# Experts in interleaved group order, and the first 128 rows of three experts computed beside the routing of the last tile

## The chip, the cores and the metric

One core of a Trainium2 chip. The metric is device time in microseconds (us) of one execution of the program; lower is better.

## What is computed

One layer over 4096 prompt tokens and 128 sample tokens of width 1024, in float32: a norm, one input projection, a Mamba-2 scan beside a gated MLP, an output projection with residual, then a mixture of experts. Its routing decides the order of everything at the end of the program:

```python
g_sel = jnp.argmax(g_logits, axis=-1)                       # 1 of 4 groups
top_val, top_idx = lax.top_k(e_sel_logits, TOP_K_IN_GROUP)  # 2 of the 8 experts of that group
weights = p_group * jax.nn.softmax(top_val, axis=-1)
expert_idx = g_sel[:, None] * EXPERTS_PER_GROUP + top_idx
# per expert, in blocks of 128 rows:
(silu(xb @ w_gate[e]) * (xb @ w_up[e])) @ w_down[e]         # 1024 -> 256 -> 1024
x = x + moe                                                 # then a last RMSNorm
```

Both experts of a token lie in one group. With these inputs the 8448 (token, expert) pairs fill 79 blocks of at most 128 rows over 32 experts.

## The kernel before

**Phase 1** (`pe_phase1`, `over_tiles`) goes over 33 tiles of 128 tokens; tile 32 is the sample (T = 4224 rows). Each turn projects tile i+1 and finishes tile i. The order on each engine is written out by hand, with semaphores between engines. For a finished tile the kernel stores the residual rows x2 and the normed rows h2 in DRAM; `dve_route` picks the two experts, `pe_rank` and `dve_slots` give each pair a slot, and `pool_scatter` writes token number and weight into that slot of `slot_d`, which has a list of T slots for each expert. The two last turns are `tn.sample` (turn 32) and `tn.end` (turn 33): no projection is left, so PE has only the output projection of the sample (L457), the ranks (L525, L526) and the updates of the sample's states (L549, `pe_sample_update`, eight pieces).

**The tables** (`dve_tables`) can be made only when the last tile has its ranks: from the counts (`carry`) VectorE works out how many blocks each expert has, which list row each of the blocks reads (`row_i`, then one gather `list_rows`), and for each block the slot of its weights in SBUF (`tcol`, `tab`). PE turns both by transposes (`pe_table_rows`, L1685 and L1692).

**Phase 2** (`over_pairs`) goes over the blocks, 80 here, in order of experts 0 to 31. A block b is: `gather(b)` of 128 rows of h2 by POOL; the transpose of those rows, made by ACT and DVE (`move`, `turn`), except for blocks 0 and 1, whose rows PE transposes itself (`pe_rows`, L1639); gate and up products (`pe_gate_up`, L1657, 8 matmuls written, 16 in the trace, in two halves); `silu` and `gate`; the transpose of the hidden rows (`pe_hidden`, L1667) and its copy (`hidden`, L1744); `pe_down` (L1676); `weigh` (L1797) on DVE, which scales by the routing weight and adds the residual row. A token's first expert writes its sum back into the x2 rows by `keep(b)`, and its last one reads it by `earlier(b)`, adds it (`add_first`, L1805), takes the last norm (`squares`, `root_of`, `norm`, L1791) and stores the row (`store`). PE's step b does gate and up of block b+1 around the hidden rows of block b, then the down product of b, so the last step also computes gate and up of a block 80 that nobody uses.

POOL issues all gathers and scatters. Its step b: `keep(b-1)`, `residual(b+1)`, `gather(b+5)`, `root_of`, `earlier(b)`, `store(b-2)`. `earlier(b)` waits until `keep(b-1)` has landed, since a row it reads can have been written by any block before. SP loads the weights of an expert (2 MB gate and up, 1 MB down) into one of four slots (`sp_phase2`), and in phase 1 the first three (`load_first`). DVE's step b: `weigh(b-1)`, `turn(b+2)`, `gate(b+1)`, `norm`, `add_first(b-1)`.

## Time and profile before

| | before |
|---|---|
| median of 3 runs | 2767.61 us (2767.44 to 2770.74) |
| the profiled execution | 2770.37 us |
| its span, first to last instruction | 2768.6 us |
| mean granted clock of TensorE | 0.993 |
| busy: PE, DVE, ACT, POOL | 2719.4, 1916.3, 1453.6, 818.5 us |

The span is what the rows of the trace lie in; the 1.8 us between it and the execution's time belong to its start and end. PE is TensorE's matmuls, PEld its weight loads, DVE is VectorE, ACT ScalarE, POOL GpSimd, SP the engine that issues most plain DMAs. A granted clock of 1.0 is 2.4 GHz, 0.5 is 1.2 GHz. "idle before <-releaser" is the time that an engine stood still before an instruction, and what ended it.

### The profile page before, as it was taken

The numbers are of one execution on the slowest core, as the hardware profiler recorded it, in microseconds if no ns is written. First come the engines' busy times: TensorE is split into PE (matmuls) and PEld (weight loads), VectorE is DVE, ScalarE is ACT, GpSimd is POOL, SyncE is SP. The second block draws the span as 40 slices with busy tenths as digits, with TensorE's granted clock in tenths as the row PEclk, the third lists the DMA queues.
The fourth block names the chain that finished last, engine by engine and source line by source line (L and its number), as shares of the span: only waits on it lengthen the run. The fifth ranks groups of instructions, "written<-read, shape, count | busy, mean of one in ns | idle before, by whom it ended". The sixth has DMA issues, their size and how long they took to land.

```text
span 2768.6 us, 38299 instructions
## 1 busy us (share of the span) xinstructions
PE 2719.4 (98%) x11649; PEld 1761.8 (64%) x11649; DVE 1916.3 (69%) x5154; ACT 1453.6 (53%) x3363; POOL 818.5 (30%) x1368
## 2 busy tenths in 40 slices
PE   8999999999999999999999999997999999999997
PEld 6777777767777777677767776773444444444443
DVE  5777777776777776767777767675666666666665
ACT  2445444554455445544554455444666666666665
POOL 1021112111211121112111211113565655656655
PEclk9999999999999999999999999998999999999999
DMA  8212211211121112111221121157888677778864
GB/s 322 94 62 77 62 46 47 77 62 46 47 76 62 47 47 77 61 47 47 72 66 46 46 76 62 50 197 281 302 285 293 239 264 267 280 256 294 319 212 145
DMA packets 109137, 377.90 MB, mean 136 GB/s; under 512 B 37201, under 2 KB 38866, under 8 KB 98930
## 3 DMA queue, kind: packets, MB, share of 16 engines
q1 hardware_dynamic: 48450, 236.13, 24.2%
q0 software_dynamic: 60480, 139.24, 15.0%
q8 instruction: 102, 1.67, 0.3%
q14 instruction: 105, 0.86, 0.1%
HBM read 326.14 MB, written 123.03 MB: 162 GB/s over the span
## 4 chain that ended last, share of the span: by engine, by line
PE 94%; DVE 2%; DMA 2%; issue 1%; ACT 1%; SPq 0%; POOL 0%; DVEq 0%; POOLq 0%; ACTq 0%
PE PB L369 24%; PE PB L1657 20%; PE PB L380 16%; PE PB L457 11%; PE SS L1676 5%; PE TB L1676 5%; PE YB L457 4%; PE YB L411 2%; DMA arena<-in_w_in 1%; PE SS L420 1%; PE SS L424 1%; PE TB L433 1%; PE YB L1667 1%; PE MB L402 1%; DVE xc L817 0%
## 5 line engine op out<-in xcount | busy, mean ns | idle before, releaser
L369 PE MATMUL PB<-arena,hT 128*128 128x512 f32 (+2 forms) x2112 | 727.7, 498 | 3.5 <-DVE x_res L937 2.2
L1657 PE MATMUL PB<-arena,hT 128*128 x1296 | 582.5, 592 | 0.0
L369 PEld LDWEIGHTS PB<-arena,hT 128*128 128x128 f32 x2112 | 397.7, 191 | 272.0 <-issue 222.4
L380 PE MATMUL PB<-hT,arena 128*128 128x128 f32 x4224 | 487.7, 277 | 4.7 <-DVE arena L1146 4.7
L380 PEld LDWEIGHTS PB<-hT,arena 128*128 128x128 f32 x4224 | 482.2, 193 | 8.6 <-issue 4.9
L1657 PEld LDWEIGHTS PB<-arena,hT 128*128 128x128 f32 x1296 | 240.2, 190 | 271.0 <-issue 271.0
L1183 POOL TENSOR_SCALAR rs<-sq 128x2 f32<-128x2 f32 (+1 forms) x66 | 14.0, 213 | 1238.5 <-ACT h L744 886.5
L457 PE MATMUL PB<-arena,tT 128*128 128x274 f32 (+1 forms) x1056 | 358.0, 493 | 0.3 <-ACT tT L638 0.3
L457 PEld LDWEIGHTS PB<-arena,tT 128*128 128x128 f32 x1056 | 195.6, 190 | 139.7 <-issue 120.5
L1787 DVE TENSOR_TENSOR gv<-ycat,PB 128x256 f32<-128x256 f32 x81 | 34.1, 421 | 288.9 <-ACT ycat L1739 288.9
L817 DVE SCALAR_TENSOR_TENSOR xc<-xT,cols,xc 128x128 f32<-128x128 f32 x792 | 216.8, 346 | 3.5
L744 ACT ACTIVATE h<-x_res 128x1024 f32<-128x1024 f32 x33 | 34.9, 1056 | 297.5 <-DVE x_res L937 297.5
L1744 ACT ACTIVATE xdt<-YB 128x256 f32<-128x256 f32 x80 | 30.6, 383 | 280.8 <-PE YB L1667 280.8
L630 ACT ACTIVATE yb<-ycat 32x128 f32<-32x128 f32 x384 | 118.1, 308 | 52.5 <-DVE ycat L928 48.4
L1676 PE MATMUL TB<-arena,xdt 128*128 x320 | 143.9, 592 | 0.0
L1676 PE MATMUL SS<-arena,xdt 128*128 x320 | 143.8, 592 | 0.0
L590 ACT ACTIVATE xT<-PB 128x512 f32<-128x512 f32 x64 | 38.3, 598 | 198.9 <-PE PB L380 198.2
L630 ACT ACTIVATE zz<-ycat 32x128 f32<-32x128 f32 x384 | 117.8, 307 | 35.1 <-DVE ycat L906 30.9
L1731 ACT ACTIVATE zz<-x_in 32x256 f32<-32x256 f32 x320 | 132.1, 413 | 3.9
L457 PE MATMUL YB<-arena,tT 128*128 128x274 f32 x528 | 127.6, 394 | 0.0
L1553 POOL DMA_INDIRECT xT<-x_rows,bc x81 | 98.7, 1219 | 68.6 <-DMA x_rows<-x_res,bc 43.6
L815 DVE TENSOR_SCALAR xc<-xT,cols 128x128 f32<-128x128 f32 x264 | 70.8, 342 | 66.2 <-issue 66.2
(292 smaller groups left out, 4204.1 us busy)
## 6 DMA issues: line engine op xcount, KB each, us to landing
arena<-in_w_expert SPq DMA_DIRECT2D x32, 2048.0 KB, 9.9
arena<-in_w_expert SPq DMA_DIRECT2D x32, 1024.0 KB, 6.5
h_rows<-h SPq DMA_DIRECT2D x34, 512.0 KB, 6.0
x_in<-in_x_rows SPq DMA_DIRECT2D x33, 512.0 KB, 4.3
hT<-in_x_cols SPq DMA_DIRECT2D x33, 512.0 KB, 3.7
x_res<-in_x_rows SPq DMA_DIRECT2D x33, 512.0 KB, 3.5
dec<-running_sums SPq DMA_DIRECT2D x33, 512.0 KB, 3.8
x_rows<-x_res SPq DMA_DIRECT2D x33, 512.0 KB, 5.2
```

Source lines behind the costliest of these rows:

```text
L369: mm = nc.tensor.matmul(out, hT[u][:, k, :], w_group(name)[:, k, :], start=k == 0, stop=k == KD - 1)
L380: mm = nc.tensor.matmul(PB[b][:, c * P:(c + 1) * P], w_block(name, c)[:, k, :], hT[u][:, k, :], start=k == 0, stop=k == KD - 1)
L411: mm = nc.tensor.matmul(bank[:, c], decay[:, h, :], xdt[:, c], start=True, stop=True)
L457: mm = nc.tensor.matmul(out_p[b], tT[:, k, :], w_out_sb[b][:, k, :], start=k == 0, stop=k == KD - 1)
L590: ins = nc.scalar.activation(xT[u][:, half(b), HALO:], PB[b][:, :].rearrange("p (k t) -> p k t", k=4), ACT.Copy)
L630: ins = nc.scalar.activation(rows_moved[b][32 * q:32 * (q + 1), g * P:(g + 1) * P], rows_quarter(b, g, q), ACT.Copy)
L815: ins = V.tensor_scalar(dst, src, tap[:, w, c:c + 1], cols[:, R_CBIAS + c:R_CBIAS + c + 1], ALU.mult, ALU.add)
L817: ins = V.scalar_tensor_tensor(out=dst, in0=src, scalar=tap[:, w, c:c + 1], in1=dst, op0=ALU.mult, op1=ALU.add)
L1553: nc.gpsimd.indirect_dma_start(out=out, out_offset=None, in_=dram, bounds_check=last, oob_is_err=False, in_offset=bass.IndirectOffsetOnAxi ...
L1657: mm = nc.tensor.matmul(PB[u][:, :], hT[u][:, k, :], arena[:, bass.ds(slot + k * 2 * DE, 2 * DE)], start=k == 0, stop=k == KD - 1)
L1676: mm = nc.tensor.matmul(dn_bank[b % 2][n], hTb[:, k, :], arena[:, bass.ds(slot + KD * 2 * DE + k * D + n * 512, 512)], start=k == 0, stop= ...
L1731: ins = nc.scalar.activation(moved[g][32 * q:32 * (q + 1), :], quarter(b, g, q), ACT.Copy)
```

## The change

1. Experts are numbered in turn over the groups: position 0, 1, 2, 3 are the first experts of groups 0 to 3, then their second ones. The host permutes router columns, biases and expert weights by `turns`; `dve_route` views the 32 logits as (expert, group). The first three positions are then of three different groups, so no token is in two of them, and each is its token's first expert.
2. The lists of those three positions have at least 128 entries after 31 tiles. While the last tile is routed, SP reads the first 128 entries of each (`early`), POOL gathers their rows (`pool_early_rows`, `pool_early_residuals`), and PE takes them as blocks 0, 1 and 2, with weights whose slots are known beforehand. Their rows are transposed on PE (`pe_rows`), copied by ACT (`act_rows`). The tables count from block 3 on; rows of the three experts beyond 128 follow as further blocks, so there are still 79 blocks and one empty one.
3. PE's step b does gate and up of block b around the hidden rows of block b-1, then the down product of b-1; the last block's hidden rows and down product stand behind the loop. The gate and up product of a block 80 is gone.
4. POOL's step: keep, residual, root, earlier, store, and `gather(b+5)` last. DVE's step: gate, weigh, turn, norm, add. The `earlier` and `store` of blocks 0 to 2 fall away.
5. Smaller: `pe_sample_update` uses two PSUM banks in place of three; the packing of the sample's convolution tail goes ahead of `act_ysq` of the sample; y, x2 and first-sum buffers change places; a few more small DVE instructions in the tables.

```diff
+EARLY = 3
-NBLK = 2 * T // P + NE
+NBLK = 2 * T // P + NE + EARLY + 1
...
             if tn.sample:
+                for b in range(2):
+                    pe_rows(pe, b)
+                pe.wait_ge(s["gx_out"], 2)
                 pe_turned(pe, i)
...
         def pe_end(pe):
             pe_sample_update(pe, 0, 2)
+            pe.wait_ge(s["x2_part"], 3 * NP + 2)
+            pe_gate_up(pe, 0, (SLOT_AT[0], 32), 0, KD)
             pe_rank(pe, NT, False, NT)
-            pe.wait_ge(s["lg_read"], NT)
-            pe_sample_update(pe, 2, 3)
+            pe_rows(pe, 2)
+            pe_gate_up(pe, 1, (SLOT_AT[1], 64), 0, KD)
...
             if tn.sample:
+                for b in range(2):
+                    act_rows(act, b)
                 act_turned(act, i)
...
             if i == CLOSED:
                 for e in range(EARLY):
                     V.tensor_scalar(carry[:, e:e + 1], carry[:, e:e + 1], float(T * e + P), None, ALU.max)
...
             if tn.to_sample:
+                dve.wait_ge(early_loaded, 16)
+                V.tensor_copy(tok_i[:, 0:EARLY], early[:, :, 0])
+                V.tensor_copy(wt[:, 0:EARLY], early[:, :, 1]).then_inc(s["early_ready"], 1)
...
             if tn.to_sample:
+                pool_early_rows(pool)
                 pool_y_root(pool, st, NP)
+                pool_early_residuals(pool)
...
             if tn.to_sample:
+                sp.wait_ge(scattered, 32 * CLOSED)
+                sp.dma_start(early[:, :, :], slot_d[0:EARLY * T, :].rearrange("(e t) a -> t e a", e=EARLY)[0:P, :, :]).then_inc(early_loaded, 16)
...
+        def pool_early_rows(pool):
+            pool.wait_ge(s["early_ready"], 1)
+            pool.wait_ge(h2_stored, 16 * (CLOSED + 1))
+            pool.wait_ge(s["cb_done"], NT)
+            pool.wait_ge(s["dec_ready"], NT)
+            for b in range(2):
+                rows_of(h2_d[0:CLOSED * P, :], g_buf[b], tok_i, b, gathered[b], CLOSED * P - 1)
+            pool.wait_ge(s["ydiag_done"], NT)
+            rows_of(h2_d[0:CLOSED * P, :], g_buf[2], tok_i, 2, gathered[2], CLOSED * P - 1)
...
             def step(b):
-                if b > 0:
-                    keep(b - 1)
+                if b < EARLY:
+                    return
+                keep(b - 1)
                 residual(b + 1)
-                gather(b + AHEAD)
-                if b > 1:
-                    pool.wait_ge(s["fin_sq"], b - 1)
-                    root_of(b % 2, b - 1)
+                n = b - 1 - EARLY
+                if n > 0:
+                    pool.wait_ge(s["fin_sq"], n)
+                    root_of(b % 2, n)
                 earlier(b)
-                if b > 1:
-                    pool.wait_ge(s["fin_out"], b - 1)
+                if n > 0:
+                    pool.wait_ge(s["fin_out"], n)
                     store(b - 2)
+                gather(b + AHEAD)
...
         def pe_phase2(pe):
+            pe.wait_ge(s["hb_ready"], 1)
+            pe_hidden(pe, 0)
+            pe.wait_ge(s["gx_out"], 3)
+            pe.wait_ge(s["hbT_out"], 1)
+            pe_down(pe, 0, SLOT_AT[0])
             pe_table_rows(pe)
+            pe_gate_up(pe, 2, (SLOT_AT[2], 96), 0, KD)
+            pe_sample_update(pe, 2, 8)
+            pe.wait_ge(s["hb_ready"], 2)
+            pe.wait_ge(s["lists_out"], 2)
+            pe_hidden(pe, 1)
+            pe.wait_ge(s["smp_new"], 8)
+            pe.wait_ge(s["hbT_out"], 2)
+            pe_down(pe, 1, SLOT_AT[1])
...
+            used = over_pairs(pe, step)
+            pe.wait_ge(s["hb_ready"], 2 * used)
+            pe_hidden(pe, 2 * SURE - 1)
+            slot = pe.value_load(final_slot, min_val=0, max_val=SLOT_AT[2])
+            pe.wait_ge(s["hbT_out"], 2 * used)
+            pe_down(pe, 2 * SURE - 1, slot)
...
         def dve_phase2(dve, st):
             def step(b):
-                if b > 0:
-                    weigh(1 - b % 2, wt[:, b - 1:b])
-                turn(b + 2)
-                gate(b + 1)
+                gate(b)
+                weigh_block(b - 1)
+                turn(b + 2)
-                if b > 1:
-                    norm(b % 2, f_buf[b % 2], b - 1)
-                if b > 0:
+                if b - 2 >= EARLY:
+                    norm(b % 2, f_buf[b % 2], b - 1 - EARLY)
+                if b - 1 >= EARLY:
                     add_first(b - 1)
```

How the edits move instructions, at the two places that the prediction speaks of. First PE, from the last piece of the sample's output projection ahead of the transition to the first gate and up product of the loop. Before (L358 turns the sample's ycat, L457 is the output projection, L525 and L526 rank a tile, L549 updates the sample's states, L1685 and L1692 turn the tables and lists, L1639 turns rows of blocks 0 and 1):

```order
L457 MATMUL YB<-arena,tT 128x274 x8
L358 MATMUL TB<-cst,ycat 128x128 x8
L457 MATMUL PB<-arena,tT 128x512 x8
L457 MATMUL PB<-arena,tT 128x274 x8
L525 MATMUL MB<-oh,cst 128x32
L526 MATMUL MB<-oh,cst 128x32
L457 MATMUL YB<-arena,tT 128x274 x8
L549 MATMUL SS<-arena,xw 128x512 x2
L525 MATMUL MB<-oh,cst 128x32
L526 MATMUL MB<-oh,cst 128x32
L549 MATMUL YB<-arena,xw 128x512
L1685 MATMUL MB<-cst,tcol 1x128 x4
```

Now (L1741 turns rows, L1759 is gate and up, L1768 and L1776 are hidden and down, L1785 and L1790 the tables):

```order
L1741 MATMUL TB<-cst,xc 128x128 x8
L1741 MATMUL TB<-cst,dec 128x128 x8
L361 MATMUL TB<-cst,ycat 128x128 x8
...
L555 MATMUL SS<-arena,xw 128x512 x2
L1759 MATMUL PB<-arena,hT 128x512 x8
L531 MATMUL MB<-oh,cst 128x32
L532 MATMUL MB<-oh,cst 128x32
L1741 MATMUL TB<-cst,x_in 128x128 x8
L1759 MATMUL PB<-arena,hT 128x512 x8
L1768 MATMUL YB<-cst,gv 128x128 x2
L1776 MATMUL TB<-arena,xdt 128x512 x4
L1785 MATMUL MB<-cst,tcol 1x128 x4
L1790 MATMUL YB<-cst,gu 128x128 x2
L1759 MATMUL PB<-arena,hT 128x512 x8
```

Two gate and up products and one down product now stand ahead of the tables' transposes, a third gate and up product right behind them, and the transposes of two blocks' rows ahead of the sample's own.

Second POOL, one step of the loop. Before (x_rows<-x_res is keep, xT or bc<-x_rows the residual, xc<-h_rows the gather, the two rs rows the root, the next read of x_rows `earlier`, out_y `store`):

```order
L1558 DMA x_rows<-x_res,bc 4352x1024
L1553 DMA xT<-x_rows,bc 128x1024
L1553 DMA xc<-h_rows,bc 128x1024
L1586 TENSOR_SCALAR rs<-sq 128x1
L1588 TENSOR_TENSOR rs<-rs,cst 128x1
L1553 DMA xT<-x_rows,bc 128x1024
L1558 DMA out_y<-arena,bc 4224x1024
```

Now:

```order
L1619 DMA x_rows<-x_res,bc 4352x1024
L1614 DMA xT<-x_rows,bc 128x1024
L1677 TENSOR_SCALAR rs<-sq 128x1
L1679 TENSOR_TENSOR rs<-rs,cst 128x1
L1614 DMA arena<-x_rows,bc 128x1024
L1619 DMA out_y<-arena,bc 4224x1024
L1614 DMA dec<-h_rows,bc 128x1024
```

The gather has moved from the place behind keep and residual to the end of the step, right ahead of the next keep.

## Rows read from the trace of the kernel before

**Rows 1.** Timeline of PE, turns 32 and 33: start us, us, engine, line, what
```profile
1855.05 1.04 PE L358 MATMUL TB<-cst,ycat 128*128 128x128 f32 x8
1856.43 10.81 PE L457 MATMUL PB<-arena,tT 128*128 128x512 f32 x32 [0.34 <-ACT tT L638]
...
1871.22 1.88 PE L549 MATMUL SS<-arena,xw 128*128 128x512 f32 x4
1879.79 0.64 PE L525 MATMUL MB<-oh,cst 128*128 128x32 f32 x2 [6.69 <-DVE oh L1079]
...
1889.49 1.01 PE L1685 MATMUL MB<-cst,tcol 128*1 128x128 f32 x4 [6.77 <-DVE tcol L1482]
1891.67 0.70 PE L1692 MATMUL PB<-cst,gu 128*128 128x128 f32 x2 [1.17 <-DMA gu<-slot_tokens,row_i]
1893.81 3.78 PE L549 MATMUL SS<-arena,xw 128*128 128x512 f32 x4 [1.44 <-DVE arena L1130]
...
1901.94 1.12 PE L1639 MATMUL TB<-cst,x_in 128*128 128x128 f32 x8 [0.42 <-ACT hT L1722]
```

**Rows 2.** Windows: PE, PEld, DVE, ACT, POOL busy, granted clock, DMA share, GB/s
```profile
1885.00:1890.00 5.00, 0.51 (x3) 0.34 (x4) 4.52 (x27) 0.00 (x0) 0.99 (x1) 0.50 0.58 181
```

**Rows 3.** Chain that ended last, first blocks of phase 2: start us, us, what
```profile
1934.40 0.22 PE YB L1667 x2
1934.62 3.44 PE PB L1657 x8
```

**Rows 4.** Timelines of DVE and ACT in the same stretch
```profile
1842.15 2.07 DVE L871 TENSOR_TENSOR x_in<-dec,cbm 128x512 f32<-128x512 f32 x2
...
1864.25 9.43 ACT L752 ACTIVATE arena<-arena,st_dec 128x128 f32<-128x128 f32 x32
```

**Rows 5.** Timeline of SP's issues, and DMA issues of 1800 to 1930 us to landing
```profile
1843.19 0.34 SPq L1275 DMA_DIRECT2D arena<-in_w_expert  x1
...
x_in<-h_rows,bc POOLq DMA_INDIRECT x4, 7.5
```

**Rows 6.** Timeline of POOL, one step of phase 2 without a wait for keep
```profile
2322.71 0.99 POOL L1558 DMA_INDIRECT x_rows<-x_res,bc  x1 [1.24 <-DVE x_res L1797]
...
2325.34 1.02 POOL L1553 DMA_INDIRECT x_in<-h_rows,bc  x1 [0.30 <-issue]
...
2327.47 1.06 POOL L1553 DMA_INDIRECT xT<-x_rows,bc  x1 [0.20 <-issue]
2330.79 1.21 POOL L1558 DMA_INDIRECT out_y<-arena,bc  x1 [2.26 <-DVE arena L1791]
```

**Rows 7.** Timeline of DVE, the same step
```profile
2328.35 0.42 DVE L1787 TENSOR_TENSOR gv<-ycat,PB 128x256 f32<-128x256 f32 x1 [3.68 <-ACT ycat L1739]
...
2331.02 1.40 DVE L1797 SCALAR_TENSOR_TENSOR x_res<-TB,bc 128x512 f32<-128x512 f32 x2
...
2333.39 1.80 DVE L1780 STREAM_TRANSPOSE hT<-xc 32x256 f32<-32x256 f32 x4
```

**Rows 8.** Waits of 1960 to 2740 us: us in total, times, longest
```profile
POOL xT L1553 <- DMA x_rows<-x_res,bc: 39.6, 18, 5.5
POOL arena L1553 <- DMA x_rows<-x_res,bc: 25.6, 11, 4.3
```

**Rows 9.** Timeline of POOL, keep and `earlier` of one step that waits
```profile
2596.26 0.99 POOL L1558 DMA_INDIRECT x_rows<-x_res,bc  x1 [1.01 <-DVE x_res L1797]
...
2603.67 2.05 POOL L1553 DMA_INDIRECT xT<-x_rows,bc  x1 [2.85 <-DMA x_rows<-x_res,bc]
```

**Rows 10.** Chain that ended last, at the end of the span
```profile
2737.64 3.43 PE SS L1676 x8
```

**Rows 11.** Timeline of DVE, the end of the span
```profile
2750.91 1.22 DVE L1805 TENSOR_TENSOR arena<-x_res,arena 128x1024 f32<-128x1024 f32 x1
2755.81 0.06 DVE L1833 MEMSET spare<- 128x1 f32 x1 [3.68 <-issue]
...
2756.14 1.41 DVE L1797 SCALAR_TENSOR_TENSOR x_res<-TB,mv,bc 128x512 f32<-128x512 f32 x2
```

More of the change, by code:

```diff
@@ L979, in dve_turn @@
                 dve_slots(dve, st, i)
+            if i == CLOSED:
+                for e in range(EARLY):
+                    V.tensor_scalar(carry[:, e:e + 1], carry[:, e:e + 1], float(T * e + P), None, ALU.max)
             if tn.prev:
@@ L1519, in sp_phase2 @@
             sp.wait_ge(s["smp_new"], 8)
-            for n in range(2):
-                sp.wait_ge(gathered[n], 16)
+            sp.wait_ge(gathered[EARLY], 16)
             sp.dma_start(ssm_sample.rearrange("p (q b n) -> p q b n", q=SB, b=4), st_old).then_inc(ssm_stored, 16)
@@ L1609, in pool_phase2 @@
             pool.wait_ge(x2_stored, 16 * NT)
-            pool.wait_ge(convp_stored, 16)
             pool.wait_ge(spill_set, 16)
-            residual(0)
+            keep(0)
+            residual(2)
+            pool.wait_ge(first_kept, 16)
+            keep(1)
+            residual(3)
+            gather(EARLY + GB)
+            pool.wait_ge(first_kept, 32)
+            last_n = last_counts(pool)
             used = over_pairs(pool, step)
-            last_n = (pool.value_load(misc[0:1, 4:5], min_val=2 * SURE - 1, max_val=2 * PAIRS - 1), 2 * used)
             for u in range(2):
@@ L1650, in pe_gate_up @@
                 pe.wait_ge(w_loaded, loads)
[L1651 to L1654 removed]
+                if b < EARLY:
+                    pe.wait_ge(s["gx_out"], b + 1)
+                else:
+                    pe.wait_ge(s["rows_turned"], b - EARLY + 1)
                 after(pe, s["hb_ready"], b - 1)
@@ L1713, in pe_phase2 @@
-            over_pairs(pe, step)
-        def act_phase2(act):
-            act.wait_ge(x2_stored, 16 * NT)
-            act.wait_ge(s["lists_out"], 2)
-            act.wait_ge(s["tables"], 1)
-            def rows0(b):
-                act.wait_ge(s["gx_T"], 2 * b + 1)
-                nc.scalar.activation(hT[b][:, half(0), :], TB[0][:, :, :], ACT.Copy).then_inc(s["gx_out0"], 1)
+                if b < EARLY:
+                    return
+                weights = pe_weights(pe, b)
+                slot = SLOT_AT[b - 1] if b - 1 < EARLY else entry(pe, TAB_SLOT, b - 1, 0, SLOT_AT[2])
@@ L1750, in step @@
             def step(b):
+                if b < EARLY:
+                    return
+                silu(b)
+                move(b + 2, 6, 12)
                 hidden(b)
-                if b > 1:
-                    squares(b % 2, f_buf[b % 2], b - 1)
+                if b - 2 >= EARLY:
+                    squares(b % 2, f_buf[b % 2], b - 1 - EARLY)
                 move(b + 3, 0, 6)
-                silu(b + 1)
-                move(b + 3, 6, 12)
-            rows0(0)
-            rows0(1)
             silu(0)
-            move(2, 0, 12)
+            act_rows(act, 2)
+            silu(1)
+            hidden(0)
+            silu(2)
+            move(3, 0, 12)
+            hidden(1)
+            move(4, 0, 12)
+            hidden(2)
+            move(5, 0, 6)
+            act.wait_ge(s["tables"], 1)
+            last_n = last_counts(act)
             used = over_pairs(act, step)
-            last_n = (act.value_load(misc[0:1, 4:5], min_val=2 * SURE - 1, max_val=2 * PAIRS - 1), 2 * used)
             squares(0, f_buf[0], last_n[0])
```

262 lines of the change are left out of this document (143 added, 119 removed).

## Prediction

> **What bounds the kernel now.** I read the page first: PE is busy for 2719 of 2769 us, so 49 us are idle. The chain of waits then says where: in phase 2 it stays on PE, round after round. A product of gate and up is twice 3.44 us, the hidden rows 0.22 and the down product 3.43, so a block costs 10.5 us of PE, and 80 of them 841 us [rows 3, 10]. No wait of PE stands in between. The timeline of PE in turns 32 and 33 holds the rest: 0.34, 6.69, 6.77, 1.17, 1.44 and 0.42 us of idle time, 16.8 in all, first for the routing of the sample on DVE, then for the tables, then for the list gather [rows 1]. In that stretch the granted clock falls to 0.5, its level of 1.2 GHz, after PE has stood idle [rows 2], and what PE does there takes twice its time: two pieces of the states' update need 3.78 us, where two pieces at full clock need 1.88 [rows 1]. The last views are those of the end: from the end of the last useful product of gate and up at 2737.6 [rows 10] to the end of the span at 2768.6 lie 31 us, most of them DVE, ACT and POOL finishing two blocks.
>
> **The transition, part by part.** I compare one event in both programs: the end of gate and up of block 3. By then both have done the same blocks' work (gate and up of 0 to 3, hidden rows of 0 to 2, down of 0 and 1). Before, it lies at 1934.62 + 3.44 = 1938.1 [rows 3], 83.0 us after PE began to turn the sample's ycat at 1855.05 [rows 1].
> - Idle time filled: -16.8.
> - Slow clock: the eight updates took 10.6 us where 8 x 0.86 = 6.9 would do; ranks and transposes of the tables, 2.6 us in all, would take about 1. With PE kept busy from here on I take the clock as full: -5.3 together. If it fell as before, this stays; so the term is 0 to -5.3, and I take the end that the busy stretches show.
> - A third block's rows are transposed on PE, and each in one go of 8: +0.7, from 1.12 us for eight [rows 1].
> - New waits of PE. Blocks 0 and 1 share one PSUM tile and each is copied by ACT in one instruction of 1024 columns (2 x 0.6 us less one start, about 1.1) before the next transposes: 2 x 1.2. The hidden rows of block 0 wait for silu(1) and their own copy: about 0.9. The down product of block 1 waits behind `move(3)` on ACT, which needs the first gather of the loop: about 1. With the copy of ycat as before: +4.5 in all. Bounds: 2 (copies hidden) and 9 (each a wait as long again).
>
> Sum: 83.0 - 16.8 - 5.3 + 0.7 + 4.5 = 66.1 us, so block 3's product would end at 1921.2, **16.9 us earlier**.
>
> What covers this? The rows of blocks 0 and 1 must be there at 1855. The lists are read behind the tile's running sums on SP and used by DVE only after its decays are made, at 1842.15 + 2.07 = 1844.2 [rows 4], so POOL issues the gathers from 1844.6 on. They share the DMA engines with 3 MB of weights issued at 1843.2; four such gathers landed in 7.5 us (median) in the same stretch [rows 5]. First gather: landed at 1852, second: about 1855. Just in time. The two turned blocks stand ahead of the sample's own rows on PE and ACT, so everything behind moves by about 4.2 us: squares of tile 31, its routing, the 9.43 us of ACT scaling the states [rows 4], the norm and routing of the sample, the tables and the list gather. I expect the last rank at 1884 where it was at 1879.8, and the tables' transposes at 1897 where they began at 1889.5. PE no longer waits there, since gate and up of block 0, then of block 1 and the down product of block 0 lie before them (6.9 + 6.9 + 3.4 = 17 us against 6.69 + 6.77 of idle time and the 4.2). On ACT the three silus and copies go between small things; on DVE `gate(0)` and `gate(1)` add 0.42 each ahead of h2 and the tables' end. The list of small table instructions (about six more at 0.15 to 0.2) is inside the 4.2 + 1 us. SP's small DMA for the lists stands ahead of waits that come later anyway: nothing. Interleaving by itself costs nothing on PE: 79 blocks before and after.
>
> **The end.** DVE's last in-loop `add_first` ends at 2750.91 + 1.22 = 2752.1, 14.5 us behind the last useful product; it stood behind `gate(80)`, which waited for the needless product. Now the down product of block 78 ends at +3.4, weigh and turn take 4.2 (2331.02 to 2333.39 + 1.80 [rows 7]), then DVE waits about 1.4 for the root, norm and add take 2.4: +11.6. What follows (3.68 us at the way out of the branches, three memsets, the last weigh at 2756.14 and 12.5 us to the end [rows 11]) stays. **2.9 us earlier.** That PE saves 7 us of product there is worth no more, since DVE's chain is the later one. Bounds: 0 (POOL's round has slipped) and 6.2 (what PE gains: 13.95 - 7.75).
>
> **The loop.** PE's order is unchanged, and it is the bound. But POOL's step is tighter. Before, between keep and `earlier` stood residual, gather and root, 4.76 us (2322.71 to 2327.47), which hid most of keep's flight; then 3.3 us later came store, and another 2 us later the next keep [rows 6]. In 29 of some 74 steps keep had not landed, and POOL waited for 65.2 us in all, 2.25 on average, 5.5 at most [rows 8]; such a step had 7.4 us from keep to `earlier` [rows 9]. Now the gather comes behind store. A round is the flight plus `earlier` (1.4), store (1.3) and gather (1.3): it fits into 10.5 us while the flight is below 6.5, that is for waits up to 1.9. A late keep also makes root, norm and add late, and those now stand on DVE ahead of the next gate. Gate had 3.68 us of slack in front [rows 7]; of it norm and add take 2.4, so with what PE's half product allows a slip of some 1.7 us is free, and waits over 3.6 reach PE. For the longest ones that is 5.5 - 3.6 and so on, some 4 us over three or four steps, and where waiting steps follow each other slips add up: I take **+6 us**. Bounds: 0 (flights get shorter with an even issue) and +27 (below).
>
> **Sum:** -16.9 - 2.9 + 6 = -13.8 against the profiled execution's 2770.4, of whose time 2768.6 is span; the median of the runs is 2.8 us below it, and I take the difference from the median: 2767.6 - 13.8 = **2753.8**. A measurement here tells 0.2%, 5.5 us, from no change.
>
> **The rivals.**
> - *The loop costs nothing.* For it: 45 of 74 steps never waited, and PE has no idle time in 780 us. Then 2767.6 - 19.8 = 2747.8.
> - *The cover in turn 32 is missing.* Gathers of blocks 0 and 1 land late behind the weights, or ACT's copies delay the routing chain by more than the blocks' products cover. Against it: the estimate above has both landed at 1855, but with no margin. Each microsecond goes straight to PE; some 6 us: 2760.
> - *POOL becomes the bound of the last third: slower.* Before, the late experts of a group, whose tokens nearly all read an earlier sum and store a final row, came in four stretches; interleaved, the late experts of all groups are the last 26 blocks. There keep would wait in every step, with a gather now right ahead of it. The step that waits 2.85 us [rows 9] has a flight of 7.4 us; with it a round is 7.4 + 4.0 = 11.4, 0.9 over PE's. If the gather ahead lengthens it by its issue distance in part, to 1.05 over, 26 rounds cost 27 us: 2767.6 - 19.8 + 27 = 2774.8. It decides from flights of 7.3 us on average there (19.8 / 26 = 0.8 over 6.5).
>   The Trainium skill, DMA: Bandwidth & Descriptors, section "Queues, rings and completion order", says that on each DMA engine descriptors are consumed in ring order. By that rule a keep starts only behind the gather and store issued ahead of it, which makes this rival more likely than the mean wait alone would; no row before shows a gather right ahead of a keep. With it in full the time would be this rival's 2774.8, without it the forecast's 2753.8.
> - *The early blocks don't run early.* Were a semaphore of the chain (list, gather, weights) late by a full transfer, PE would wait as before with the blocks behind it: no gain but the end's 2.9, 2764.7. Against it: all three weights are loaded in turn 31 to 33 already.
>
> **How the numbers follow.** Forecast 0.42, no cost in the loop 0.27, cover missing 0.14, POOL the bound 0.12, not early 0.05. The range of 8 in 10: from 2744 (no cost in the loop, and 4 us of the bounds of transition and end on top) to 2766 (a loop that costs 18). Faster by over 0.2% is below 2762.1: nearly all of the first two and most of the third, 0.82. Slower by over 0.2%, above 2773.1: most of the fourth, 0.09. Within: 0.09. The forecast alone has 2748 to 2760.
>
> **What would show it.** Gate and up of block 3 ends near 1921 in the chain; PE's idle time between 1855 and 1921 is below 6 us, at a granted clock of 1.0 throughout. The last rank is at 1884, the list gather's transposes are no wait. In the loop the waits list has new rows, PE waiting for DVE's gate (the hidden rows) in a few steps, and POOL's waits for keep grow; most of both lie in the last third. From the last gate and up to the span's end it is 28 us, not 31. I am wrong if PE waits at 1855 for gathered rows, if the last rank comes later than 1888, or if the idle time of PE in the loop is far from 6 us: near 0 the second part of my sum was needless, above 20 POOL has become the bound.

## The result, and the profile after

The changed kernel is slower, by less than 2% but clear of the noise. Its 13 runs have a median of 2819.08 us and lie between 2782.32 and 2852.60 us; 13 runs of the kernel before have a median of 2769.66 us and lie between 2767.44 and 2772.79. The ratio of the two is 1.0108, with a 95% interval of 1.0074 to 1.0142. It is made from the lower runs of the changed kernel, because the comparison leaves out those more than 1.5% above its fastest; the medians of all runs are 1.8% apart. The spread is itself a result: 5 us before, 70 us after. The profiled execution is the median one, 2819.08 us.

The page of the changed kernel, its first lines and its chain of waits (busy time and share of the span by engine; then the chain's shares by engine and by line):

```profile
span 2817.2 us, 38181 instructions
...
PE 2727.5 (97%) x11641; PEld 1761.4 (63%) x11641; DVE 1910.9 (68%) x5159; ACT 1447.1 (51%) x3339; POOL 804.3 (29%) x1356
...
PE 77%; DMA 11%; issue 6%; POOL 3%; DVE 2%; POOLq 0%; SPq 0%; ACT 0%; DVEq 0%; ACTq 0%
PE PB L372 24%; PE PB L383 16%; PE PB L460 12%; DMA x_rows<-x_res,bc 10%; PE PB L1759 9%; PE YB L460 4%; PE SS L1776 2%; PE TB L1776 2%; PE YB L414 2%; DMA arena<-in_w_in 1%; PE SS L423 1%; PE SS L427 1%; PE TB L436 1%; POOL x_in L1614 1%; POOL out_y L1619 1%
```

PE still looks busy for 97% of the span, and a reader who stops there would see nothing wrong. The chain says otherwise: 11% of it is DMA, and 10% is one line, the keep (`x_rows<-x_res`). A transfer now stands in the chain that sets the end.

I cut the span at the two events that the prediction used, the end of gate and up of block 3 and the end of the last useful gate and up. The chain gives both for the kernel after:

```profile
1921.37 0.22 PE YB L1768 x2
1921.59 3.43 PE PB L1759 x8
...
2780.33 3.44 PE PB L1759 x8
2783.76 3.45 PE TB L1776 x8
```

| us | before [rows 3, 10] | after | difference |
|---|---|---|---|
| end of block 3's gate and up | 1938.1 | 1925.0 | -13.0 |
| from there to the last useful gate and up | 799.6 | 858.7 | +59.2 |
| from there to the end of the span | 31.0 | 33.4 | +2.5 |
| span | 2768.6 | 2817.2 | +48.6 |

So the early blocks bring their gain, the end costs a little, and the expert loop loses 59 us where 6 were forecast.

The transition, in the timeline of PE (start us, us, engine, line, what, in brackets the idle time before and its releaser), answers to [rows 1]:

```profile
1858.99 1.07 PE L1741 MATMUL TB<-cst,dec 128*128 128x128 f32 x8 [1.21 <-ACT hT L753]
1861.17 1.52 PE L361 MATMUL TB<-cst,ycat 128*128 128x128 f32 x8 [1.11 <-ACT hT L753]
...
1887.22 0.30 PE L531 MATMUL MB<-oh,cst 128*128 128x32 f32 x2
...
1896.36 3.67 PE L1776 MATMUL TB<-arena,xdt 128*128 128x512 f32 x8 [0.62 <-ACT xdt L1852]
...
1913.95 3.70 PE L1776 MATMUL SS<-arena,xdt 128*128 128x512 f32 x8 [0.57 <-DVE arena L1154]
```

The two waits of 6.7 us are gone: directly before the last rank (L531) there is no idle time. The four waits that are left between 1855 and 1921 make 3.5 us.

The windows of the loop show where PE lost time (columns: stretch, its length, PE busy, granted clock, DMA share, GB/s); before, all five stretches were full:

```profile
1950.00:2100.00 150.00, 125.68 (x298) 0.96 0.70 251
2100.00:2250.00 150.00, 150.00 (x371) 1.00 0.77 259
2250.00:2400.00 150.00, 150.00 (x372) 1.00 0.78 266
2400.00:2550.00 150.00, 138.14 (x332) 0.98 0.74 249
2550.00:2700.00 150.00, 142.04 (x343) 0.98 0.79 274
```

The loss begins with the first blocks of the loop, stops for 300 us and comes back twice. Where PE stands idle the mean granted clock sinks as well, to 0.96 and 0.98. Over the whole loop, from the end of block 3's gate and up to that of the last useful one:

```profile
1925.00:2783.80 858.80, 814.41 (x1978) 0.98 0.75 257
```

PE stood still for 44.4 us. Before, the same work took 799.5 us at a clock of 1.00 without any idle time, so the other 15 us of the 59 are products that ran at the lower of the two clock levels: the granted clock has six stretches of 3.4 us and one of 6.8 at 0.50 there, and half their length is 14 us.

The waits of 1960 to 2740 us (us in total, times, longest) answer to [rows 8]:

```profile
POOL bc L1614 <- DMA x_rows<-x_res,bc: 133.1, 29, 8.3
POOL arena L1614 <- DMA x_rows<-x_res,bc: 103.8, 28, 8.4
...
DVE arena L1887 <- POOL rs L1679: 269.1, 68, 8.7
PEld YB L1768 <- DVE gv L1480: 60.2, 21, 6.9
PE YB L1768 <- DVE gv L1480: 44.4, 17, 6.1
```

POOL waits for the keep for 237 us in 57 steps, where it was 65 us in 29. What follows is a ladder: DVE waits for the root that POOL could not make (up to 8.7 us), the gate stands behind that norm in DVE's order, and PE's hidden rows wait for the gate: 44.4 us in 17 blocks, which is all the idle time that PE has in the loop. (The row of PEld shows the weight load ahead of the same products; it is not to be added.)

One POOL round shows the mechanism, and answers to [rows 6, 9]:

```profile
1965.25 1.03 POOL L1619 DMA_INDIRECT x_rows<-x_res,bc  x1 [0.30 <-issue]
1966.58 1.03 POOL L1614 DMA_INDIRECT xT<-x_rows,bc  x1 [0.31 <-issue]
1967.68 0.19 POOL L1677 TENSOR_SCALAR rs<-sq 128x1 f32<-128x1 f32 x1
1967.96 0.56 POOL L1679 TENSOR_TENSOR rs<-rs,cst 128x1 f32<-128x1 f32 x1
1976.12 1.06 POOL L1614 DMA_INDIRECT arena<-x_rows,bc  x1 [7.59 <-DMA x_rows<-x_res,bc]
1977.49 1.02 POOL L1619 DMA_INDIRECT out_y<-arena,bc  x1 [0.30 <-issue]
1978.81 1.02 POOL L1614 DMA_INDIRECT x_in<-h_rows,bc  x1 [0.31 <-issue]
1980.14 1.03 POOL L1619 DMA_INDIRECT x_rows<-x_res,bc  x1 [0.30 <-issue]
```

From keep to keep it is 14.89 us. 10.87 of them lie between keep and `earlier`: the keep landed 10.1 us behind its issue, and `earlier` starts 0.77 us behind the landing, here as in every other round that waits. Then 4.02 us go to `earlier`, store and gather, back to back. PE needs 10.5. Nothing in this round waits for PE or DVE any more: POOL and the keep's flight set the pace.

### The profile page after: what moved, and what is told of

Its sections match the earlier page's. It is cut to its first block, busy times and chain, and to the rows that moved or that the text cites. A ratio compares the mean times of both kernels' runs of the same rounds, so it can differ in the third digit from the quotient of the medians.

```text
span 2817.2 us, 38181 instructions
## 1 busy us (share of the span) xinstructions
PE 2727.5 (97%) x11641; PEld 1761.4 (63%) x11641; DVE 1910.9 (68%) x5159; ACT 1447.1 (51%) x3339; POOL 804.3 (29%) x1356
## 4 chain that ended last, share of the span: by engine, by line
PE 77%; DMA 11%; issue 6%; POOL 3%; DVE 2%; POOLq 0%; SPq 0%; ACT 0%; DVEq 0%; ACTq 0%
PE PB L372 24%; PE PB L383 16%; PE PB L460 12%; DMA x_rows<-x_res,bc 10%; PE PB L1759 9%; PE YB L460 4%; PE SS L1776 2%; PE TB L1776 2%; PE YB L414 2%; DMA arena<-in_w_in 1%; PE SS L423 1%; PE SS L427 1%; PE TB L436 1%; POOL x_in L1614 1%; POOL out_y L1619 1%
## 5 line engine op out<-in xcount | busy, mean ns | idle before, releaser
L1759 PE MATMUL PB<-arena,hT 128*128 (+1 forms) x1280 | 585.5, 601 | 0.0
L1759 PEld LDWEIGHTS PB<-arena,hT 128*128 128x128 f32 x1280 | 241.0, 193 | 275.3 <-issue 275.3
L1887 DVE SCALAR_TENSOR_TENSOR arena<-arena,rs 128x1024 f32<-128x1024 f32 x76 | 97.6, 1284 | 284.7 <-POOL rs L1679 284.7
L1776 PE MATMUL SS<-arena,xdt 128*128 (+1 forms) x320 | 144.1, 593 | 1.1 <-DVE arena L1154 0.6
L1776 PE MATMUL TB<-arena,xdt 128*128 (+1 forms) x320 | 143.9, 592 | 0.6 <-ACT xdt L1852 0.6
L460 PEld LDWEIGHTS YB<-arena,tT 128*128 128x128 f32 x528 | 99.9, 189 | 22.1
```

What stands on the lines that cost most here:

```text
L460: mm = nc.tensor.matmul(out_p[b], tT[:, k, :], w_out_sb[b][:, k, :], start=k == 0, stop=k == KD - 1)
L1759: mm = nc.tensor.matmul(PB[u][:, :], hT[u][:, k, :], arena[:, bass.ds(slot + k * 2 * DE, 2 * DE)], start=k == 0, stop=k == KD - 1)
L1776: mm = nc.tensor.matmul(dn_bank[b % 2][n], hTb[:, k, :], arena[:, bass.ds(slot + KD * 2 * DE + k * D + n * 512, 512)], start=k == 0, stop= ...
L1887: V.scalar_tensor_tensor(out=rows, in0=rows, scalar=rs[:, u:u + 1], in1=gf_b, op0=ALU.mult, op1=ALU.mult).then_inc(s["fin_out"], 1)
```

## The experiments

My theory after this reading (A): the gather's place on POOL does it. It lay in the shadow of the keep's flight, and stands behind the wait now; and the keep is issued as the fourth transfer in a row. Rival B: the interleaved order bunches the traffic. Rival C: DVE's new order, norm and add ahead of the gate, hands every delay to PE.

**1. The gather put back behind the residual, nothing else.**

```diff
                 residual(b + 1)
+                gather(b + AHEAD)
                 n = b - 1 - EARLY
...
-                gather(b + AHEAD)
```

> The changed kernel, with only the gather of block b+5 put back where it stood before: right behind the residual and ahead of the root, so inside the time that the keep is in flight. Theory A (the order on POOL's queue): the changed kernel loses some 60 us in the expert loop because each POOL round is now the keep's flight plus three issues (earlier, store, gather, 4.02 us), and because the keep is queued right behind a gather and so flies 8 to 11 us. Put back, the round is one issue (1.34 us) shorter and the keep has the gather behind it instead of ahead: the mean wait of POOL for the keep falls from 8.3 to under 5 us, TensorE's waits for DVE's gate mostly go, time 2755 to 2770 us. Theory B (interleaved experts bunch the traffic or put blocks in other neighbourhoods, which makes keep and residual slower whatever the order): waits stay at 8 us, time over 2800 us. Theory C (the lag-2 order in DVE's step, norm and add ahead of the next gate): POOL's waits fall but the time does not, 2800 us or more.

Measured: 2757.64 us (2756.97 to 2758.95), ratio to the kernel before 0.9958 (0.9942 to 0.9975). One line moved gives 61 us back by the medians, and some 41 (1.5%) by the two ratios. The waits of 1960 to 2740 us, and the same stretch of POOL:

```profile
DVE arena L1887 <- POOL rs L1679: 202.4, 74, 4.3
POOL bc L1614 <- DMA x_rows<-x_res,bc: 41.4, 15, 4.1
POOL arena L1614 <- DMA x_rows<-x_res,bc: 31.4, 16, 3.7
```

```profile
1969.14 0.98 POOL L1619 DMA_INDIRECT x_rows<-x_res,bc  x1 [2.40 <-issue]
1970.43 1.04 POOL L1614 DMA_INDIRECT xT<-x_rows,bc  x1 [0.30 <-issue]
1971.78 1.01 POOL L1614 DMA_INDIRECT xc<-h_rows,bc  x1 [0.30 <-issue]
1972.86 0.19 POOL L1677 TENSOR_SCALAR rs<-sq 128x1 f32<-128x1 f32 x1
1973.13 0.56 POOL L1679 TENSOR_TENSOR rs<-rs,cst 128x1 f32<-128x1 f32 x1
1977.54 1.06 POOL L1614 DMA_INDIRECT bc<-x_rows,bc  x1 [3.85 <-DMA x_rows<-x_res,bc]
1978.90 1.01 POOL L1619 DMA_INDIRECT out_y<-arena,bc  x1 [0.30 <-DVE x_res L1486]
```

In this long round it is 8.40 us from keep to `earlier` (the keep flew 7.6, the longest of the stretch), and the next keep goes at 1980.22: 8.40 + 2.68 = 11.1 us, and the round before took 10.54. PE's wait for the gate is gone from the list. Theory A holds for the loss, B and C predicted no gain. DVE still stands in the new order here, so that order costs PE nothing in this kernel.

The flights differ too, and that was not in my sum. The keeps' DMA to landing, between 1950 and 2100 us, in the kernel after and then with the gather put back:

```profile
DMA to landing us min/median/max: 6.4/9.5/10.3
```

```profile
DMA to landing us min/median/max: 3.7/5.0/7.6
```

It was 3.0/5.8/8.1 in the kernel before. It would be rash to put the whole of this down to the three issues ahead of the keep: in the changed kernel itself the order is the same between 2100 and 2250, and there the landings are

```profile
DMA to landing us min/median/max: 3.9/4.8/7.8
```

Experiment 6 comes back to this.

**2. The wait for the keep relaxed.** In the interleaved order a token's two experts are at least four experts apart, so `earlier` of block b needs the keep of b-2 at most. The keeps count on two semaphores by parity.

```diff
-                after(pool, first_kept, 16 * b)
+                after(pool, first_kept[b % 2], 16 * (b // 2))
```

> The changed kernel, in which the earlier of block b waits for the keep of block b-2 instead of b-1 (the keeps count on two semaphores by parity; in the interleaved order a token's two experts lie at least four experts apart, so the rows of block b were kept before b-1). The wait for a flight leaves POOL's round altogether. Theory A (round of POOL = keep's flight + 4 us): the waits of POOL for x_rows fall from 250 us to under 60 us, the rounds fall to TensorE's pace, time 2745 to 2762 us. Theory B (bunched traffic makes the transfers themselves slow): the waits move to the gathered rows or to the residual, 2790 us or more. Theory C (order in DVE's step): 2800 us or more, with DVE's waits for the root unchanged at 8 us.

Measured: 2757.84 us (2754.69 to 2759.44), ratio 0.9955 (0.9938 to 0.9971). No wait of POOL for `x_rows` is left in the loop, the rounds have a median of 10.52 us (9.7 to 11.4), and DVE waits 3.0 us at most for its root, although the gather stands last as in the change and the keep's median landing is 7.5 us (6.5/7.5/8.6 between 1950 and 2100, of the seven keeps there whose landing is on record). A long flight costs nothing once no one waits for it at once.

**3. Both.**

> Both: the earlier of block b waits for the keep of b-2, and the gather of b+5 stands behind the residual as before. Theory A: with the flight off POOL's round the gather's place no longer matters, so this equals the kernel with the relaxed wait alone within 0.3%, 2745 to 2762 us. If the place of the gather alone sets how long the norm waits for its root (the reason of the move), it is slower than that kernel by up to 1.3 us a block, some 10 us or more. Theory B or C: 2790 us or more.

Measured: 2760.10 us (2757.17 to 2760.49), ratio 0.9962 (0.9948 to 0.9976). As fast as either, within the noise. The norm's wait for its root is 4.3 us at most instead of 3.0: the move of the root does what it says, and it brings nothing, since PE hardly waits for DVE in either (0.3 us in one block here).

**4. Interleaving alone**, on the kernel before.

> The kernel before, with only the experts in interleaved group order (weights, router columns and the mask's layout), nothing begun early and POOL's step as it was. Theory A (POOL's order) says nothing is lost by it: 2765 to 2775 us. Theory B (interleaving itself slows keeps and residuals in the loop): 2800 us or more, with POOL's waits for keeps at 7 to 8 us instead of some 2.

Measured: 2770.54 us (2767.28 to 2772.00), ratio 0.9998 (0.9989 to 1.0008). Its longest wait for a keep is 3.8 us. Rival B is out.

**5. The gather between root and `earlier`.**

```diff
                     root_of(b % 2, n)
+                gather(b + AHEAD)
                 earlier(b)
...
-                gather(b + AHEAD)
```

> The changed kernel with the gather between the root and the earlier: the root still stands ahead of the gather, as the change wants it, but the gather lies inside the keep's flight. If what costs 60 us is only that the gather stands behind the wait for the keep (theory A), this is as fast as the kernel with the gather put back behind the residual: 2754 to 2762 us, with the norm's mean wait for its root at 3.0 to 3.6 us instead of 4.3. If the move of the root ahead of the gather is itself harmful, 2770 us or more.

Measured: 2757.01 us (2754.89 to 2762.34), ratio 0.9968 (0.9954 to 0.9982), and two later kernels with this order gave 0.9956 and 0.9953. The root stands ahead of the gather, the norm waits 3.0 us at most, the keep's shadow is filled. It beats the kernel before and the changed one, and differs from the change by one line.

**6. The gather last, alone**, in the kernel before.

```diff
                 residual(b + 1)
-                gather(b + AHEAD)
...
                     store(b - 2)
+                gather(b + AHEAD)
```

> The kernel before, with only POOL's gather moved to the end of its step (behind earlier and store). Theory A: that alone is enough to lose what the change lost in the loop, without early blocks, without interleaving and with DVE's old order: POOL's mean wait for the keep rises from some 4 to over 7 us, TensorE waits for DVE's gate or for the rows, time 2800 to 2840 us. If it needs the interleaved order or DVE's new order with it: below 2785 us.

Measured: median 2800.91 us over 10 runs from 2769.24 to 2851.11, ratio 1.0091 (1.0062 to 1.0120). No early block, no interleaving, DVE's old order, and a loss of the same kind with the same spread. Its size is smaller: 31 us by the medians, against the 61 of experiment 1, and the shortest run loses nothing. The profiled run is one of the shorter ones, 2778.8 us, and shows the loss as it begins; POOL's mean wait is 3.1 us, not the 7 that I expected. Its waits of 1960 to 2740 us, and the first stretch in which PE loses time:

```profile
POOL xT L1553 <- DMA x_rows<-x_res,bc: 89.2, 30, 6.5
POOL arena L1553 <- DMA x_rows<-x_res,bc: 79.4, 24, 6.9
```

```profile
2550.00:2700.00 150.00, 143.29 (x344) 0.98 0.72 249
```

So the waits of the whole loop had grown, from 65 to 169 us, and PE was reached only after 2550. The keeps of 1950 to 2100 here:

```profile
DMA to landing us min/median/max: 3.3/5.2/8.4
```

Each of these 14 keeps goes out 0.30 us behind the gather, with no other pause, exactly as in the changed kernel, where the median of this stretch is 9.5. So the order of the issues is one part of the flight and not the whole. The other part is in the transfer records: the weights that SP loads meanwhile, which are all that its queue carries in the loop. Sorted by the KB that SP's queue began in the 5 us behind the keep's issue (keeps of 1960 to 2740; median flight in us, number of keeps):

```
weights in these 5 us   before     gather put back   changed kernel   before, gather last
under 200 KB            2.9 (24)   2.8 (22)          4.4 (31)         4.3 (47)
200 to 600 KB           5.0 (16)   4.1 (6)           6.8 (15)         6.5 (18)
over 600 KB             5.8 (34)   5.8 (45)          8.0 (23)         8.1 (8)
```

At equal weight traffic the two kernels with the gather last agree, and so do the two with it behind the residual. The gather's place lengthens the flight by 1.5 us without weights and by 2.2 beside over 600 KB (the middle row has few keeps), and the weights by 3 to 4. No run moves the loads by themselves, so this second part is read from the traces and not tested. In the changed kernel a 2 MB load is issued beside every second keep from 1980 on (1980.55, 2006.87, 2033.88 and 2058.31 us, keeps at 1980.14, 2007.23, 2033.85 and 2060.25). In this profile the 2 MB loads are issued about 3 us behind a keep (1978.12, 1999.16 and 2030.73, keeps at 1975.10, 1996.14 and 2027.71), and most of the weights have passed before the next one. Where the loads fall may also be why runs of one program differ by 70 us. That is not shown, since each kernel has one profile.

**7. The end of the span.** In the changed kernel POOL's last instruction ends at 2808.1, and the span at 2817.2; before it was 2766.3 and 2768.6. No transfer and no instruction of another engine lies in the 9 us. The records show POOL in a DRAIN, the closing one of its program. Seven kernels ask what sets it. Two issue more small indirect DMAs:

```diff
+            if i <= 3:
+                for k in range(2):
+                    nc.gpsimd.indirect_dma_start(out=slot_d[:, :], ...).then_inc(extra, 16)
+                pool.wait_ge(extra, 32 * i)
```

> The changed kernel with the gather put back, plus six more small indirect DMAs on POOL in phase 1 (the two scatters of the first three tiles are issued twice), so that POOL issues 472 of them as the kernel before does, where the changed kernel issues 466. In the records POOL's closing DRAIN takes 2.3 us in both kernels with 472 and 9.1 to 9.2 us in all three with 466. Theory D (what the drain takes depends on how many indirect DMAs POOL has issued): the drain is back at 2.3 us and the run is 6.8 us faster than the kernel with the gather put back, about 2750.8 us. Theory E (it depends on the code at the end, which reads two counts more): drain 9.2 us, time 2757.6 us.

> The same with two more scatters (468 indirect DMAs). Theory D: the drain changes in a regular way with the count, so it lies between, some 4.5 to 7 us, or at 2.3 if the count only has to be a multiple of four. Theory E: 9.2 us.

Measured: drains of 9.23 us in both, 2759.53 us (ratio 0.9963, 0.9951 to 0.9976) and 2757.71 us (0.9962, 0.9947 to 0.9976). Theory D is wrong in this form. Next, the code at the end and the number of written steps:

```diff
-            last_n = last_counts(pool)
             used = over_pairs(pool, step)
+            last_n = last_counts(pool)
...
-                pool.wait_ge(y_stored[u], 16 * stores[u])
+                pool.wait_ge(y_stored[u], 8 * last_n[u] + 8 * u)
```

> The changed kernel with the gather between root and earlier, and POOL's code around the end as in the kernel before: the counts are loaded behind the loop, and the waits for the last stores take their numbers from them instead of from two more loads. In the run with 472 indirect DMAs POOL's closing DRAIN still took 9.2 us, so the count is not what sets it. Theory E1 (those loads at the end make the drain long): drain 2.3 us, time 2750 us. Theory E2 (the two more pairs of steps that the change lets the code be written for, 50 instead of 48) and theory E3 (something else): drain 9.2 us, time 2757 us.

```diff
-NBLK = 2 * T // P + NE + EARLY + 1
+NBLK = 2 * T // P + NE
```

> The changed kernel with the gather between root and earlier, and with NBLK = 96 as before instead of 100: steps for 48 pairs of blocks are written instead of 50, of which 40 run. E2: POOL's drain falls to 2.3 us, time 2750 us. E1 or E3: 9.2 us and 2757 us.

> The kernel before with NBLK = 100 instead of 96, nothing else. E2: POOL's drain rises from 2.3 to 9.2 us, time 2776 us. E1 or E3: 2.3 us and 2769.5 us.

Measured: 2757.05 us, 2756.96 us and, from the kernel before, 2769.30 us; drains 9.24, 9.23 and 2.29 us. E1 and E2 are out. Last, as many full-sized indirect DMAs as before:

```diff
+                if b in MORE:
+                    after(pool, extra, 16 * MORE.index(b))
+                    rows_of(h2_d[:, :], flat(tT[:, :, :]), tok_i, b, extra, T + P - 1)
```

> The changed kernel with the gather between root and earlier, and six more indirect DMAs of full size (128 rows of 4 KB, read into a tile that is free by then, at blocks 20, 24, ... 40). The change issues six such DMAs fewer than the kernel before (three earliers, three stores); the six extra scatters of the other run were small ones (32 packets instead of 144). The drains measured so far are 2.12, 2.29, 9.07 and 9.23 us, which are 13, 14, 55 and 56 times 0.164 us. Theory D2 (what the drain takes goes by the descriptors that POOL has issued since its queue was last cleared up, and starts again from near nothing when that comes round): with as many as before the drain is 2.3 us and the time about 2750.5 us. Theory E3 (something else in the changed program): 9.2 us, time 2757 us.

> The same with one more full-sized indirect DMA, at block 20. Theory D2: one step of 0.164 us more, so the drain is 9.39 us, or already round again at 2 us or less. Theory E3: 9.23 us as in the kernel without it.

Measured: 2756.72 us (ratio 0.9958, 0.9942 to 0.9975) with a drain of 8.82 us, and 2756.15 us (0.9954, 0.9938 to 0.9971) with 9.23. D2 is out as well: 60480 packets on the queue, exactly as many as before, and no short drain. All of them side by side:

```
kernel                        indirect DMAs  written pairs  POOL's closing DRAIN, us
before                        472            48             2.29
interleaved only              472            48             2.29
before, gather last           472            48             2.12
before, NBLK 100              472            50             2.29
changed kernel                466            50             9.07
gather put back               466            50             9.23
wait relaxed                  466            50             9.07
both                          466            50             9.23
gather between                466            50             9.23
 and code of the end          466            50             9.24
 and NBLK 96                  466            48             9.23
 and one more, full size      467            50             9.23
 and six more, full size      472            50             8.82
gather put back, two small    468            50             9.23
gather put back, six small    472            50             9.23
```

None of the edits brings the short drain back; the most that one does is 0.4 us (8.82 with six more of full size). What is left is what all changed kernels share and these edits left alone, such as the early blocks and the loop that begins at block 3. The cause stays open.

## Why the prediction was wrong

Forecast 2753.8 us in a range of 2744 to 2766; measured 2819.1. Step by step:

**The transition was right.** The forecast for the end of block 3's gate and up was 1921.2. With the gather put back it is 1921.1, with the gather between 1919.8, in the changed kernel 1925.0. The last rank was forecast at 1884; it stands at 1883.3, 1882.0 and 1887.2 in the same three. The idle time of PE between 1855 and 1921 is 3.5 us, below the 6 that I named. That one kernel agrees to 0.1 us is luck, since the kernels with this transition spread over 5 us. What differs most is the clock in the window ahead of all this, where PE had no idle time: ahead of the fall it ran narrow products of 8 and 64 columns, in both. After, then with the gather between (granted clock 0.50, which is 1.2 GHz, and 1.00), each with the row of PE that runs in it:

```profile
1845.00:1850.00 5.00, 5.00 (x18) 0.50 0.99 415
```

```profile
1847.19 6.03 PE L460 MATMUL PB<-arena,tT 128*128 128x274 f32 x16
```

```profile
1845.00:1850.00 5.00, 5.00 (x25) 1.00 0.98 409
```

```profile
1845.28 3.92 PE L460 MATMUL PB<-arena,tT 128*128 128x274 f32 x16
```

The kernel with interleaving alone shows the low level there too (0.52 in this window), so it is no property of the early blocks. "With PE kept busy from here on I take the clock as full" held for the long stretch at 0.50 of [rows 2], which none of the changed kernels has: all of them show 1.00 from 1870 to 1925. Short falls ahead of it remain. The four kernels with the early blocks and the low level at 1845 end block 3's gate and up at 1923.5 to 1925.0, the others at 1919.8 to 1921.5. The 16.9 us forecast were 17.0 and 18.3 in the two kernels without a loss in the loop, and 13.0 here.

**The loop is the step that failed.** I wrote: "A round is the flight plus `earlier` (1.4), store (1.3) and gather (1.3): it fits into 10.5 us while the flight is below 6.5." The form of the round is right: 4.02 us plus the time from keep to `earlier`, which is what I called the flight; the flights of the experiments are to the landing, 0.77 us less, so they must stay below 5.7. What failed is the length that I put in. I took the flights of the kernel before and got +6 us. In that trace the keep had a pause ahead of it and no gather: 2.26 us ahead of the store and 1.24 ahead of the keep [rows 6]. With the gather right ahead the flight is 1.5 to 2.2 us longer at the same weight traffic (experiment 6), so that every keep beside over 600 KB of weights is over the 5.7, and in the first 150 us the loads also fell beside the keeps: 9.5 us (median) where it had been 5.8. The term is +59 us. An estimate from the record says that the longer flight alone is enough. I add up the lateness of the 75 rounds that the kernel before has between 1950 and 2740 (its flight + 0.77 + 4.02 - 10.52 us each, never below zero, and all over the 1.7 us that I had called free a loss): 7 us are lost with its own flights, close to my +6, but 48 with each 1.5 us longer and 78 with each 2.0 us longer. My bound of +27 failed for the same reason: it let keep to `earlier` be 7.4 us and charged 26 blocks late in the loop, while from 1950 to 2100 it was 10.3 (median of 11).

The rival "POOL becomes the bound" had the right mechanism, at 0.12, and the wrong place: I tied it to the late experts in the last third. The runs show that it does not need the interleaved experts: interleaving alone costs nothing (experiment 4), and the gather's place costs time without it (experiment 6). The rule that I had weighed against my sum, that descriptors are consumed in ring order (the Trainium skill, DMA: Bandwidth & Descriptors, section "Queues, rings and completion order"), agrees with the flights of 4.4 against 2.8 us where no weights are beside the keep, and should have raised that rival's chance for the whole loop. The same section says that each DMA engine takes its queues in turn, packet by packet. The transfer records agree with that here. The packets begun per us in the flight that we saw above, on POOL's queue and on SP's:

```
us      POOL's queue, KB   SP's queue (weights), KB
1967    300                  0
1968     36                208
1970     44                272
1972     48                304
1974    120                232
1976     96                312
```

As soon as weights come, POOL's queue gets a small share. In 1970, 1972 and 1974 it begins 15, 19 and 33 packets and SP's queue 17, 19 and 28, nearly the same number, but SP's are of 8 to 16 KB and POOL's of 4 KB (medians). So what is queued on POOL's then lasts long: the keep issued at 1965.25 has 512 KB and landed at 1975.4.

That waits of up to 3.6 us are absorbed by the gate's slack was right in kind: with the gather put back POOL waits 73 us in 31 steps, 4.1 at most, and PE loses nothing. It is no help against rounds that are too long one after the other.

**The end.** Forecast 28 us behind the last useful gate and up, measured 33.4. The part that I worked out held. DVE's last add in the loop ends 11.4 us behind (forecast 11.6, though the terms 3.4, 4.2, 1.4 and 2.4 that I gave add up to 11.4), the way out of the branches took 1.4 us instead of 3.68, and POOL's last instruction ends 24.3 us behind, where it was 28.6. I had left what follows as it was; it is the DRAIN, 2.3 us before and 9.1 after, 6.8 us that no row of the kernel before could show. The last rows of POOL in the changed kernel, whose span ends at 2817.2, 9.1 us behind them:

```profile
2805.25 0.99 POOL L1619 DMA_INDIRECT out_y<-x_res,bc  x1 [0.17 <-issue]
2807.91 0.19 POOL L1729 TENSOR_TENSOR spare<-cst 128x1 f32<-128x1 f32 x1 [1.66 <-DMA out_y<-x_res,bc]
```

With the loop's term at zero and the end's as measured, the prediction's transition makes a span of 2768.6 - 16.9 + 2.5 = 2754.2. The profiled execution with the gather between has a span of 2753.1 us (it is the shortest of its five runs, 2.1 us below their median), and its cuts lie at 1919.8 and 2719.6:

```profile
1916.10 0.22 PE YB L1768 x2
1916.32 3.44 PE PB L1759 x8
...
2716.20 3.44 PE PB L1759 x8
2719.63 3.45 PE TB L1776 x8
```

That is -18.3, +0.3 and +2.5 us against the kernel before: the gain of the early blocks whole, and a loop that costs nothing. The gather at the end of the step, which I priced at +6 with the old flights, was the one edit that did harm.

## What to carry to other kernels

An issue that stands between the start of a transfer and the wait for it was hidden here; behind the wait it made the round 1.3 us longer, and the transfer 1.5 to 2.2 us longer as well. Whether that costs anything depends on the room in the round: the shortest run of experiment 6 lost nothing, the longest 80 us. When a change closes the pauses on a queue, don't put the old flights into the new round, and ask what else will be under way beside each of them: keeps with a weight load beside them flew 3 to 4 us longer here. Where a wait can be for the round before the last instead of the last (experiment 2), try that first: it made the place of the gather harmless. And a spread of 70 us where there had been 5 was the mark of a loop at the edge of its budget, even when single runs still looked fast.

## What the runs showed that I had not expected

- The closing DRAIN on POOL takes 2.1 to 2.3 us in four kernels of the old family and 8.8 to 9.2 us in eleven of the new one, with nothing in flight that the profile shows. Kernels with the gather last have 0.16 us less than their nearest relatives, in both families. Neither the number and size of POOL's indirect DMAs nor the code of the end nor the number of written steps brings it back to 2.3 (one kernel with six more moved to 8.8).
- The granted clock fell to 0.50 at 1845 in some kernels while PE had no idle time, and not in others with the same instructions there; what follows lies 2 to 5 us later in those kernels, which is as much as some of the terms that one tries to predict.
- The place of one issue on POOL, which is busy for 29% of the span, is worth 61 us by the medians, 2.2% of the kernel, while interleaving all experts is worth nothing.
- The flight of the same 512 KB write goes from 2.9 us (no weights beside it) to 5.8 (over 600 KB of them in 5 us), and with a gather right ahead of it from 4.4 to 8.0.
